# Weights in transfers of two chunks: a hybrid transformer block on one Trainium2 core

## The reference, cut to what matters

```
for i in range(DEPTH):                         # DEPTH = 2
    h_l = modulate(rmsnorm(x, g_norm1[i]), sh1, sc1)       # the same for ctx
    out_l, out_c = token_mixer(h_l, h_c, w_in[i], ..., w_attn_out[i], w_four_out[i], w_gate[i], w_out[i], ...)
    x = x + ga1 * out_l
    toks = ...                                 # rmsnorm + modulate of x (and ctx in layer 0)
    y = moe(toks, w_router, b_router, w_e_gate[i], w_e_up[i], w_e_down[i])
    x = x + ga2 * y
# moe: for e in range(16):
#     he = silu(h @ w_e_gate[e]) * (h @ w_e_up[e])         # 1024 x 512 each
#     y = y + gates[:, e:e+1] * (he @ w_e_down[e])         # 512 x 1024
```

## Time and profile before

| | us |
|---|---|
| median of 3 runs (lowest, highest) | 1667.79 (1667.19, 1669.01) |
| the profiled execution | 1670.19 |
| its span, first to last instruction | 1668.5 |
| PE busy | 1481.5 (89%) |
| DVE busy | 1046.0 (63%) |
| ACT busy | 870.9 (52%) |
| POOL busy | 141.4 (8%) |

### The profile page before, as it was taken

The page is one execution under the profiler, slowest core; times in us unless marked ns, Lnnn a source line. Parts: engine busy times, 40 slices in busy tenths (PEclk is TensorE's granted clock), DMA queues, the critical chain, the costliest instruction groups (busy, mean ns, idle before and its releaser), DMA issues.

```text
span 1668.5 us, 22782 instructions
## 1 busy us (share of the span) xinstructions
PE 1481.5 (89%) x7758; PEld 1115.8 (67%) x7758; DVE 1046.0 (63%) x1515; ACT 870.9 (52%) x1307; POOL 141.4 (8%) x139
## 2 busy tenths in 40 slices
PE   5789999998879987999999739999989779999993
PEld 2577777776547846888777628988758546666662
DVE  2312344322985437999999654653486579999994
ACT  4323122223773243887777426422575457777783
POOL 1100000000000001011111010000000012232201
PEclk8799999999999996999999969999999879999997
DMA  8742666665002305999999572632405179999992
GB/s 285 275 173 102 238 235 219 212 211 207 1 30 83 122 37 199 372 394 394 394 393 393 214 250 89 213 128 90 138 1 176 63 254 380 380 382 380 376 385 96
DMA packets 179149, 373.88 MB, mean 224 GB/s; under 512 B 11633, under 2 KB 11954, under 8 KB 178434
## 3 DMA queue, kind: packets, MB, share of 16 engines
q1 hardware_dynamic: 166674, 323.20, 54.5%
q0 software_dynamic: 11536, 46.53, 7.6%
q10 hardware_dynamic: 864, 3.15, 0.5%
HBM read 346.62 MB, written 26.21 MB: 223 GB/s over the span
## 4 chain that ended last, share of the span: by engine, by line
PE 59%; DMA 17%; DVE 13%; issue 5%; ACT 4%; POOL 1%; SPq 1%; DVEq 0%; POOLq 0%; ACTq 0%
PE ps L502 16%; PE ps L503 15%; PE ps L504 15%; DMA w_raw<-in_w_e_gate 8%; DMA w_raw<-in_w_e_up 4%; PE ps L712 3%; DVE w_lo_more L498 2%; DVE amax L1410 2%; PE ps L730 2%; DMA w_raw<-in_w_gate 2%; DVE w_lo L498 2%; DMA w_raw<-in_w_in 1%; PE ps L798 1%; PE ps L818 1%; DVE att_a L1319 1%
## 5 line engine op out<-in xcount | busy, mean ns | idle before, releaser
L498 DVE TENSOR_TENSOR w_lo<-w_raw,w_hi 128x1024 fp32r<-128x1024 f32 x320 | 383.3, 1221 | 386.1 <-ACT w_hi L494 380.2
L494 ACT ACTIVATE w_hi<-w_raw 128x1024 fp32r<-128x1024 f32 x320 | 336.0, 1058 | 460.9 <-PE ps L504 163.0
L502 PE MATMUL ps<-h_hi,w_hi 128*128 128x512 f32 (+1 forms) x704 | 251.7, 358 | 18.8 <-DVE h_lo L1335 9.1
L503 PE MATMUL ps<-h_lo,w_hi 128*128 128x512 f32 (+1 forms) x704 | 248.4, 353 | 0.0
L504 PE MATMUL ps<-h_hi,w_lo 128*128 128x512 f32 (+1 forms) x704 | 248.3, 353 | 0.0
L498 DVE TENSOR_TENSOR w_lo_more<-w_raw,w_hi_more 128x1024 fp32r<-128x1024 f32 x192 | 227.5, 1218 | 13.9 <-ACT w_hi_more L494 10.2
L494 ACT ACTIVATE w_hi_more<-w_raw 128x1024 fp32r<-128x1024 f32 x192 | 200.6, 1058 | 53.9 <-DMA w_raw<-in_w_e_gate 18.1
L502 PEld LDWEIGHTS ps<-h_hi,w_hi 128*128 128x128 f32 x704 | 134.8, 192 | 44.6 <-issue 11.2
L504 PEld LDWEIGHTS ps<-h_hi,w_lo 128*128 128x128 f32 x704 | 134.8, 191 | 18.9
L503 PEld LDWEIGHTS ps<-h_lo,w_hi 128*128 128x128 f32 x704 | 134.8, 192 | 18.4 <-issue 0.2
L502 PE MATMUL ps<-w_hi,xg_hi 128*128 128x512 f32 (+1 forms) x256 | 104.9, 410 | 12.4 <-DVE xg_lo L1608 12.3
(11 more groups left out here) (237 smaller groups left out, 2546.3 us busy)
## 6 DMA issues: line engine op xcount, KB each, us to landing
w_raw<-in_w_e_gate SPq DMA_DIRECT2D x128, 512.0 KB, 7.9
w_raw<-in_w_e_up SPq DMA_DIRECT2D x128, 512.0 KB, 9.6
w_raw<-in_w_e_down SPq DMA_DIRECT2D x128, 512.0 KB, 9.0
w_raw<-in_w_ada SPq DMA_DIRECT2D x96, 512.0 KB, 5.7
w_raw<-in_w_in SPq DMA_DIRECT2D x56, 512.0 KB, 6.7
w_raw<-in_w_gate SPq DMA_DIRECT2D x32, 512.0 KB, 8.1
w_raw<-in_w_attn_out SPq DMA_DIRECT2D x16, 512.0 KB, 3.8
w_raw<-in_w_out SPq DMA_DIRECT2D x16, 512.0 KB, 3.6
```

The lines of the kernel that those rows point to most:

```text
L494: act.activation(whi(n), raw[:, slot(n), :, :], ACT.Copy).then_inc(hi_ready, 1)
L498: dve.tensor_tensor(wlo(n), raw[:, slot(n), :, :], whi(n).bitcast(F32), ALU.subtract).then_inc(lo_ready, 1)
L502: pe.matmul(acc, sh, mh, start=first, stop=False, skip_group_check=True)
L503: pe.matmul(acc, sh, ml, start=False, stop=False, skip_group_check=True)
```

## The change

Two neighbouring chunks are loaded by one transfer of 1 MB. `w_pair` takes four row blocks where `w_chunk` takes two. `load_pair` waits until both slots are free (it waits for the lo_ready of chunk n + 1), fills slots a and a + 1, and signals once, on the semaphore of the even slot. `arrival(n)` gives that semaphore to both chunks' split_hi. Layer 0's mixer keeps its single loads. For w_e_down and w_four_out, whose 512 rows are two chunks, a pair is one column half.

```diff
+    def w_pair(w, k0, n0):
+
+        return w[k0 * P:(k0 + 2 * CK) * P, n0:n0 + CW].rearrange("(k p) n -> p k n", p=P)
+
-    def chunk_of(i, s, ch):
+    def chunk_of(i, s, ch, take=w_chunk):
...
+    def arrival(n):
+
+        return raw_in[slot(n) if n < exp0[0] else slot(n) // 2 * 2]
+
+    def load_pair(sp, n, src, it=None, per=0):
+
+        if exp0[0] + WS <= n < exp0[0] + RAW:
+            sp.wait_ge(ada_used, 2 * AG * 4)
+        else:
+            sp.wait_ge(lo_ready, scaled(n + 1 - (WS if n < exp0[0] + WS else RAW) + 1, it, per))
+        a = slot(n)
+        sp.dma_start(raw[:, a:a + 2, :, :].rearrange("p s k n -> p (s k) n"), src).then_inc(arrival(n), 16)
...
     def split_hi(act, n, it=None, per=0):
-        act.wait_ge(raw_in[slot(n)], raw_value(n, it, per))
+        act.wait_ge(arrival(n), raw_value(n, it, per))
...
-                load(sp, mix0[i] + n, chunk_of(i, s, ch))
+                if i == 0:
+                    load(sp, n, chunk_of(i, s, ch))
+                elif ch % 2 == 0:
+                    load_pair(sp, mix0[i] + n, chunk_of(i, s, ch, w_pair))
...
             def weights(n, w, e, it=None):
-                for ch in range(4):
-                    k, cc = (ch % 2, ch // 2) if w is w_e_down else (ch, 0)
-                    load(sp, n + ch, w_chunk(w[i, e], CK * k, CW * cc), it, 24)
+                for ch in (0, 2):
+                    k, cc = (0, ch // 2) if w is w_e_down else (ch, 0)
+                    load_pair(sp, n + ch, w_pair(w[i, e], CK * k, CW * cc), it, 24)
```

More of the change, by code:

```diff
@@ L325, in w_chunk @@
         return w[k0 * P:(k0 + CK) * P, n0:n0 + CW].rearrange("(k p) n -> p k n", p=P)
-    def chunk_of(i, s, ch):
+    def w_pair(w, k0, n0):
+        return w[k0 * P:(k0 + 2 * CK) * P, n0:n0 + CW].rearrange("(k p) n -> p k n", p=P)
+    def chunk_of(i, s, ch, take=w_chunk):
         kind = s[0]
         if kind == "WF":
-            return w_chunk(w_four_out[i], CK * (ch % 2), CW * (ch // 2))
+            return take(w_four_out[i], CK * (ch % 2), CW * (ch // 2))
         w, n0 = {"F": (w_in[i], 3 * D), "GF": (w_gate[i], D), "QK": (w_in[i], 0), "V": (w_in[i], 2 * D),
                  "GA": (w_gate[i], 0), "WA": (w_attn_out[i], 0), "WO": (w_out[i], 0)}[kind]
-        return w_chunk(w, CK * ch, n0 + CW * s[1])
+        return take(w, CK * ch, n0 + CW * s[1])
     mix0, exp0 = [], []
```

## The result

| | before | after |
|---|---|---|
| median of 4 runs each, us | 1668.40 | 1682.83 |
| lowest to highest, us | 1667.19 to 1669.49 | 1679.56 to 1685.36 |
| profiled execution (span), us | 1670.19 (1668.5) | 1683.57 (1681.9) |

The ratio is 1.0079, with a 95% interval of 1.0064 to 1.0094 (the two medians by themselves give 1.0086). The change makes the kernel 0.8% slower. The forecast was 1671.1, its range ended at 1680, and rival B (the queue runs dry) had been priced at 1680. In all four sets in which the change was run it was slower: 1.0079, 1.0092, 1.0065 and 1.0064, on average 1.0075 or 12.5 us.

A forecast was written before the change was run, and what follows sets the result against it. The prediction took the experts to be bound by DMA, with PE 0.73 and 0.82 us per expert behind. Its terms, 2.3 + 0.95 + 1.2 - 1.1 = +3.35 us, took the median from 1667.79 to 1671.1 us; range 1661 to 1680.

The forecast's parts named there:

- rival B: Expert stretches: the load queue runs dry as second slots free over 2 us later; about +9 us, time 1680; chance 0.22.
- Step 6: A pair load's added wait on SyncE's queue: covered by queued transfers with 1.1 us left, taken as zero.
- step 2: Saturated expert stretches: one completion packet fewer per engine and pair, 3.9 ns per chunk over 285 chunks, -1.1 us.
- Step 1: SyncE issues half as many loads; issue is not a bound, counted at zero.
- Step 3: Where the chain leaves DMA in each layer's experts: one DVE split later, +1.16 us per layer, +2.3 us together.
- Step 4: Start of each layer's experts: pairs issued one split later while DMA is unsaturated, 0.6 us each, +1.2 us.
- Step 5: Layer 1's mixer start: chunks 2 and 3 arrive together, ACT does two splits before the norm, +0.95 us.
- The signs that I had set: Wrong if expert stretches change over 3 us each; pair's least issue-to-landing stays above 4.7 us, share 1.05, below 1 otherwise.
- C: Expert stretches: the excess is paid per transfer, so pairs gain 10 us, time 1658; chance 0.18.
- D: At the two exits from DMA, DVE's and PE's lead hides the delays; no change, time 1668; chance 0.15.

The follow-up runs named there:

- e2: Kernel before, but from the first expert on the first of two neighbouring single loads waits until both slots are free; ratio 0.9998.
- e3: Kernel before, but from the first expert on a split waits until both neighbouring chunks have landed, loads issued singly; ratio 1.0015.
- e1: Kernel before with single 512 KB loads, but issue waits for both slots and splits wait for both landings; ratio 1.0050.
- e9: Kernel before with single 512 KB loads, issue waiting for both slots and splits for both landings, run beside the change; ratio 1.0032.
- e13: Changed kernel with each pair sent as two 512 KB transfers on the pair's one semaphore; ratio 1.0045.
- e16: Kernel before with single 512 KB loads on two semaphores, issue waiting for both slots and splits for both landings, in a later set; ratio 1.0043.
- e4: Kernel before with each load from the first expert on issued as two 256 KB transfers on the same semaphore; ratio 1.0008.
- e7: Kernel before with w_e_down cut into chunks of 128 rows by 1024 columns, 4 KB rows, still 512 KB; ratio 0.9960, median 1663.29 us.
- e14: Changed kernel with single loads in layer 1's mixer and for gate and up weights of each layer's first two experts; ratio 1.0069 to the kernel before.
- e11: Kernel before with 1 MB pairs in layer 1's mixer alone, all experts loading singly; ratio 1.0007.
- e10: The changed kernel run once more, against the kernel before in the same set; ratio 1.0065.
- e5: The changed kernel run again, against the kernel before in another set; ratio 1.0092.

## Why the prediction was wrong

**Step 6 failed, "Taken as zero".** The predicted mechanism was in the text, as rival B. One at a time the two delays cost -0.3 us (e2) and +2.5 us (e3). Together they cost 7 us (e1, e9, e13, e16), where steps 3 to 5 had 4.45. The some 5 us that appear only when both act (the intervals of e2 and e3 are wide) go with the dry spells of the windows, and for those the step had nothing.

One reason is a number read in the wrong place. The 6.7 us of cover came from 763 to 875 us, the steady part. At 680 to 744 us, a stretch that step 2 counted as saturated, the answer for the loads of before is

```profile
DMA to landing us min/median/max: 5.0/8.2/10.0
```

With 5.0 in place of 6.7 step 6's own working is 5.0 - 3.3 - 1.16 - 1.16 = -0.6 us, below zero, and the point from which B decides had been passed. That is not the whole reason, since the changed kernel loses at 754 to 793 us too, mostly inside the stretch where the 6.7 us had been read and 1.1 us should have been left. The other is the delay of the second slot, put at 1.16 us. With a result copy between the two splits it is 1.7 us (689.6 to 691.34 us), which I had written under B, as over 2 us, and left out of the sum. And where `he` and `xg_lo` run ahead of a pair's two splits, two issues stand 4.0 us apart; that is in no step.

The steps alone gave +3.35 us; the stages measured 8.7 + 1.75 + 4.0 = +14.4 in the profiled execution, in which layer 0's mixer happened to be 1.0 us shorter; the medians differ by 14.4 as well, and over four sets it is 12.5.

**The size of the transfer** had no term. It may be worth 3 to 6 us. That is argued from medians whose intervals touch and not shown, and no run here shows a cause for it.

**Step 1** (issue costs nothing) holds: SyncE's rows show the same 373 ns per issue, and half as many.

**Step 2** (completions): the count was exact, 3,584. Its price of 7.8 ns per packet put on e4's added completions, over the 285 chunks that count, is +2.2 us; e4 measured +1.3 with an interval from -0.7 to +3.3. It fits, and so does nothing at all. e7 shows that the row length carries half to two thirds of the difference between 386 and 428 GB/s.

**Step 3** (the later signal, +2.3 us): e3, the signal alone, measured +2.5 us (-0.3 to +5.2); it holds step 5's wait as well, together +3.3. The size fits, but the place that I named did not stay: in the change the chain leaves DMA 43 us later than before in layer 0 and 30 us in layer 1 (20 when counted from the layer's first gather).

**Step 4** (the later issue at the start, +1.2): e2, the issue alone, measured -0.3 us (-2.8 to +2.0), and e14 found nothing to gain at the start. Nearer to zero than to my value.

**Step 5** (one more split ahead of the norm, +0.95): the table load begins 2.02 us after the split that the fourth chunk's landing released, before 1.08 us:

```profile
989.34 2.01 ACT L511 ACTIVATE w_hi<-w_raw 128x1024 fp32r<-128x1024 f32 x2 [1.71 <-DMA w_raw<-in_w_in]
991.36 1.28 ACT L1071 ACT_TABLE_LOAD   x1
```

From the first gather of results to the table load it is 26.53 us against 25.77, +0.76; with e11 26.11, +0.34, with e10 26.94, +1.17; e11's mixer as a whole is not longer. Right in kind, the size at the limit of what can be told.

**The signs that I had set** were half right. Both expert stages changed by more than 3 us (8.7 and 4.0), the sign that the forecast is wrong. The share fell below 1 in single microseconds, as written for B, though not over two experts (1.03). But the least time from issue to landing of a pair at 763 to 875 us stayed at 6.7 us, above my limit of 4.7, and said nothing: a pair's landing time contains its own 2.7 us of transfer and the rise of a dry queue. Only the windows show it, the short ones best. That the least time of single loads stood at 6.7 us, B's argument against itself, was no protection.

**Rivals.** B was right in mechanism and sign, and 3 us short of the first result (12.5 us over four sets are 1680). In that closeness is some luck: B put 4.3 us into layer 0 and 5.0 into layer 1, with 1.8 from steps 3 and 4 on top of each. Layer 0's experts took 8.7 us more (5.2 to 6.0 in the other three executions), layer 1's 4.0 (2.7 to 4.2), and what a 1 MB transfer may cost by itself is in the measured numbers and not in B. C fell with e4. D's slack exists (e2), but not for both delays at once.

## What to carry to other kernels

When a ring feeds an engine at its limit, count bytes in flight at the tightest place of the stage and not in its steady part: there the least time from issue to landing, less what a load needs in an empty queue, is the reserve, and every added delay (issue, signal, other work between two frees) draws on the same account. Merging two transfers is such a delay twice, even with no byte and no instruction added; where the DMA engines are already busy without a gap, lengthen the rows of a transfer (+2% in bytes per second here) before its size. A delay that costs nothing alone proves no slack for two: e2 and e3 cost 2 us in sum, together 7. And a difference of a few us between two builds is worth splitting by stage: here a part of it lay where both do the same.

## What the runs showed of the hardware

- A dry load queue takes long to fill. In e10, with its issue at 978.26 us, the windows of half a microsecond (columns as in the earlier trace rows) are

```profile
978.50:979.00 0.50, 0.00 (x0) 0.00 (x0) 0.50 (x1) 0.00 (x0) 0.00 (x0) 0.50 0.00 0
979.00:979.50 0.50, 0.00 (x0) 0.00 (x0) 0.46 (x2) 0.00 (x0) 0.00 (x0) 0.50 0.58 53
979.50:980.00 0.50, 0.00 (x0) 0.00 (x0) 0.50 (x1) 0.00 (x0) 0.00 (x0) 0.50 0.72 66
...
980.50:981.00 0.50, 0.50 (x3) 0.50 (x4) 0.00 (x0) 0.00 (x0) 0.00 (x0) 0.50 1.02 381
```

  The share is 0.58 less than 1.3 us after the issue, yet the bytes reach full rate only after 2.2 us; a high share alone is no proof of bytes. With single loads of 512 KB it is the same within a window of half a microsecond (2.4 us in e9 and before).
- Rows of 4 KB in a third of the expert weights raise the rate from 390 to 399 GB/s at the same share (e7); splitting transfers down to 256 KB changes nothing that can be told (e4).
- One transfer of 1 MB in an empty queue lands 5.14 us after its issue (e10), two of 512 KB 5.57 us after the first issue and 5.06 us after the second (e9). Whether it costs more in a full ring is open.
- Layer 0's mixer, the same work with single loads up to about 561 us, ended between 633.63 and 643.32 us in eight profiled executions (e16, e5). A difference of a few us between two kernels is not theirs until the stage is named.
